# Three of every eight weighted one-hot rows on GpSimd instead of VectorE

## The reference, cut to what matters

```python
def one_block(args):
    x_blk, i_blk, g_blk = args
    u = jnp.take(peer_u, i_blk, axis=0)
    a = jax.nn.gelu(jnp.einsum("td,thkd->thk", x_blk, u)) * g_blk
    v = jnp.take(peer_v, i_blk, axis=0)
    return jnp.einsum("thk,thkd->td", a, v)
```

## Time and profile before

| | us |
|---|---|
| median of the runs | 3234.27 |
| lowest, highest run | 3233.52, 3235.56 |
| span of the profiled execution, first to last instruction | 3233.2 |
| VectorE busy in the span | 2188.2 (68%) |
| TensorE busy | 2442.6 (76%) |
| GpSimd busy | 823.7 (25%) |
| ScalarE busy | 1107.1 (34%) |

### The profile page before, as it was taken

The page is one execution under the profiler, slowest core; times in us unless marked ns, Lnnn a source line. Parts: engine busy times, 40 slices in busy tenths (PEclk is TensorE's granted clock), DMA queues, the critical chain, the costliest instruction groups (busy, mean ns, idle before and its releaser), DMA issues. The chain is left out here.

```text
span 3233.2 us, 30451 instructions
## 1 busy us (share of the span) xinstructions
PE 2442.6 (76%) x10473; PEld 1867.0 (58%) x10473; DVE 2188.2 (68%) x3036; ACT 1107.1 (34%) x1880; POOL 823.7 (25%) x571
## 2 busy tenths in 40 slices
PE   6896999999999999999999996000034005999994
PEld 5765787888888887888778796000023004444441
DVE  3698546545454555564545558999999999565668
ACT  4434235344343445454555442000089105000000
POOL 0200000000010100000000002777766773644444
PEclk9998599999999999999999998555555558999997
DMA  8452065565656555655435564999999996999998
GB/s 241 156 169 91 7 203 176 189 195 183 193 184 194 181 195 173 201 172 176 153 122 183 175 213 185 420 397 386 393 394 394 389 404 217 376 409 410 409 409 344
DMA packets 277587, 813.19 MB, mean 252 GB/s; under 512 B 32601, under 2 KB 40001, under 8 KB 243424
## 3 DMA queue, kind: packets, MB, share of 16 engines
q1 hardware_dynamic: 203504, 408.87, 37.9%
q0 software_dynamic: 73728, 402.69, 31.4%
q10 hardware_dynamic: 240, 0.18, 0.0%
HBM read 807.48 MB, written 4.19 MB: 251 GB/s over the span
## 5 line engine op out<-in xcount | busy, mean ns | idle before, releaser
L194 DVE TENSOR_TENSOR wl<-ring,wh 128x1024 fp32r<-128x1024 f32 (+2 forms) x616 | 738.9, 1241 | 647.1 <-ACT wh L189 644.5
L189 ACT CAST wh<-ring 128x1024 fp32r<-128x1024 f32 (+2 forms) x616 | 609.7, 1040 | 702.7 <-PE ps L210 649.1
L208 PE MATMUL ps<-wh,th 128*128 128x512 f32 (+1 forms) x1632 | 641.5, 393 | 28.8 <-DVE wl L194 21.6
L1805 POOL DMA_INDIRECT expert_rows<-in_peer_u,index x256 | 481.7, 1882 | 626.7 <-PE ps L1891 437.8
L210 PE MATMUL ps<-wh,tl 128*128 128x512 f32 (+1 forms) x1632 | 634.4, 389 | 0.0
L209 PE MATMUL ps<-wl,th 128*128 128x512 f32 (+1 forms) x1632 | 634.3, 389 | 0.0
L2195 DVE CUSTOM_DVE_ANT_0 junk<-expert_rows,h 128x2048 f32<-128x2048 f32 x256 | 570.1, 2287 | 6.0 <-DMA expert_rows<-in_peer_u,index 5.1
L2218 DVE SCALAR_TENSOR_TENSOR x_and_pieces<-expert_pieces,const,x_and_pieces 128x1024 f32<-128x1024 f32 x256 | 327.8, 1283 | 170.1 <-DMA expert_pieces<-in_peer_v,piece_index 87.2
L2278 PE MATMUL ps<-expert_slabs,by_expert 128*128 128x512 f32 x1024 | 439.7, 592 | 0.7 <-ACT by_expert L2319 0.7
L208 PEld LDWEIGHTS ps<-wh,th 128*128 128x128 f32 x1632 | 308.0, 189 | 101.8 <-DVE wl L194 31.8
L210 PEld LDWEIGHTS ps<-wh,tl 128*128 128x128 f32 x1632 | 307.7, 189 | 63.6
(11 more groups left out here) (332 smaller groups left out, 2748.5 us busy)
## 6 DMA issues: line engine op xcount, KB each, us to landing
ring<-in_w_in SPq DMA_DIRECT2D x112, 1024.0 KB, 5.1
ring<-in_w_up SPq DMA_DIRECT2D x64, 1024.0 KB, 5.3
ring<-in_w_down SPq DMA_DIRECT2D x64, 1024.0 KB, 5.0
expert_slabs<-in_peer_v SPq DMA_DIRECT2D x128, 512.0 KB, 6.8
ring<-in_w_out SPq DMA_DIRECT2D x32, 1024.0 KB, 5.0
ring<-in_w_peer_q SPq DMA_DIRECT2D x16, 1024.0 KB, 5.2
ring<-in_w_ukv SPq DMA_DIRECT2D x8, 1024.0 KB, 5.3
ring<-in_w_uq SPq DMA_DIRECT2D x8, 768.0 KB, 4.6
```

The costliest lines, as they stand in the source:

```text
L189: self.nc.scalar.copy(self.wh[:, i % 2, two, 0:w], self.ring[:, i, two, 0:w]).then_inc(self.high_ready, 1)
L194: self.nc.vector.tensor_tensor(self.wl[:, i % 2, two, 0:w], self.ring[:, i, two, 0:w], self.wh[:, i % 2, two, 0:w].bitcast(F32), ALU.subtr ...
L208: mm(o, hi, wh, start=start and k == 0, stop=False)
L1805: nc.gpsimd.indirect_dma_start(p.rows[:, n % GR, :], None, peer_u, bass.IndirectOffsetOnAxis(ap=p.index[:, n:n + 1], axis=0)).then_inc(p.l ...
```

## The change

Slots 2, 3 and 7 of each round of the second half are made by GpSimd, with the same instruction and operands as on VectorE. VectorE makes the other five. GpSimd makes its three rows of round r ahead of gather r, in the same queue, for r = 0 to 15; each row waits on `hot_used` for its four slots, and round 0 also for the turned weights (`columns`) and the index row (`iota_in`). TensorE waits for these slots on a semaphore of their own. The adds, the gathers' order and the first half are as they were.

```diff
+    POOL_ROWS = (2, 3, 7)
@@ gpsimd
+            def rows_by_pool(r):
+                if r == 0:
+                    pool.wait_ge(columns, 4)
+                    pool.wait_ge(iota_in, 16)
+                for i in POOL_ROWS:
+                    n = 8 * r + i
+                    pool.wait_ge(hot_used, P + n // 4 * 4 + 4)
+                    nc.gpsimd.tensor_scalar(row_hot[:, i, :], iota, turned_keys[:, 0, n:n + 1], turned_w[:, n:n + 1],
+                                            ALU.is_equal, ALU.mult).then_inc(rows_pooled, 1)
+
             for n in range(UNITS * TOPK):
+                if n < P // 8:
+                    rows_by_pool(n)
                 if n >= GR:
                     pool.wait_ge(piece_used, n - GR + 1)
                 nc.gpsimd.indirect_dma_start(
@@ vector, rows_by_vector
                 for n in range(at, at + 4):
-                    nc.vector.tensor_scalar(row_hot[:, n % 8, :], iota, turned_keys[:, 0, n:n + 1],
-                                            turned_w[:, n:n + 1], ALU.is_equal, ALU.mult).then_inc(rows_hot, 1)
+                    if n % 8 not in POOL_ROWS:
+                        nc.vector.tensor_scalar(row_hot[:, n % 8, :], iota, turned_keys[:, 0, n:n + 1],
+                                                turned_w[:, n:n + 1], ALU.is_equal, ALU.mult).then_inc(rows_hot, 1)
@@ tensor, spread
-                pe.wait_ge(rows_hot, g * 8 + (n + 1))
+                if half and i in POOL_ROWS:
+                    pe.wait_ge(rows_pooled, g * len(POOL_ROWS) + POOL_ROWS.index(i) + 1)
+                elif half:
+                    pe.wait_ge(rows_hot, P + g * (8 - len(POOL_ROWS)) + len([j for j in range(i + 1) if j not in POOL_ROWS]))
+                else:
+                    pe.wait_ge(rows_hot, g * 8 + (n + 1))
```

More of the change, by code:

```diff
@@ L2068, in peer_stage @@
          iota_in, sums_in, x_back, gain_in, added, sums, mean_ready, rooted, normed, stored, final, piece_used,
-         pieces_indexed, slab_used) = core.new(
+         pieces_indexed, slab_used, rows_pooled) = core.new(
             "dve_done", "rows_used", "shifted", "exponentiated", "gelued", "weighted", "picks_turned",
@@ L2072, in peer_stage @@
             "sums_in", "x_back", "gain_in", "x_added", "x_sums", "mean_ready", "rooted", "normed",
-            "stored", "final_steps", "pieces_used", "pieces_indexed", "expert_slabs_used")
+            "stored", "final_steps", "pieces_used", "pieces_indexed", "expert_slabs_used",
+            "rows_pooled")
         cols_hot = core.new("cols_hot_low", "cols_hot_high")
```

## The result

The changed kernel takes 3264.94 us (median of four runs, 3263.30 to 3268.07) against 3233.89 (3233.25 to 3235.56): 31.1 us slower, ratio 1.0095 with a 95% interval of 1.0081 to 1.0110. The way was forecast and the time lies within the stated range by 1 us, but the shift is 31.1 us where 13.6 were forecast.

The account below looks back on a forecast made before the run. The tail was taken as bound by bytes, its start set by the spread. Two rounds, 8.83 + 0.64 + 0.2 = 9.67 us, or 4.84 a round, end the spread 13.6 us later: 3234.3 + 13.6 = 3247.9, 3248 us; range 3240 to 3266.

Parts of the forecast that it names:

- The mechanism: In the spread, gathers queue behind GpSimd's rows and lose their lead, making a two-round loop of 4.84 us a round.
- The loop: From TensorE's last slot through row, gather, landing, add and VectorE's rows back to TensorE: 9.67 us for two rounds.
- The failed step: In the spread's loop: slot 7's GpSimd row costs 0.5 us, and slots 2 and 3 end about 0.2 us late.
- blocking of the gather: In the spread, a gather meeting a running VectorE add waits 0 to 1.28 us, mean 0.64.
- the gather's issue and landing: In the spread's loop: issue gap 0.30 us, then landing 4.2 us counted from the gather's start.
- VectorE and TensorE with the wake-ups: In the spread's loop: wake-up 0.1 us, VectorE's add, five rows and column compare 3.08, TensorE's last two slots 0.65.
- The price of a row: One 128x128 compare on GpSimd in the spread: taken as 0.5 us, between 0.32 and 0.75.
- The third rival: In the spread, serialised ports or rows of 1.3 us give 6.35 us a round, +34.8 us, 3269; chance 0.11.
- the landing loop: Spread rounds wait for each piece's DMA landing: 4.3 to 5.5 us a round, chance 0.76.
- The tail: Pieces and slabs after the spread: ends as far behind the spread as now, so everything moves by 13.6 us.
- The faster rival: Spread rounds take 3.79 us and the 9 us blocked gather at 2745.7 goes, gaining 8 us: 3225; chance 0.04.
- The Trainium skill's port rule: GpSimd operations reading SBUF and two-input VectorE ones block each other for a whole instruction; full exclusion over 6 us a round.

Follow-up runs that it names:

- e3: Against the kernel before: VectorE makes all eight rows, GpSimd none, but gather r still waits for TensorE's use of round r - 1's slots; 3252.62 us, +18.0.
- e1: Against the changed kernel: GpSimd's three rows of round r stand ahead of gather r + 7 instead of gather r; 3254.69 us, +20.1 over the kernel before.
- e2: Against the changed kernel: GpSimd's three rows of round r stand ahead of gather r + 1 instead of gather r; 3246.9 us, +12.3 over the kernel before.
- e6: Against the changed kernel: only slots 2 and 7 on GpSimd, rows of round r ahead of gather r + 1; 3237.9 us, +3.1 over the kernel before.
- e7: Against the kernel before: two tiny VectorE writes with waits ahead of each of the eight adds behind the spread; 3230.74 us, -4.1.

## Why the prediction was right in kind and wrong in size

**The mechanism held.** VectorE waits for each second piece (5.2 to 5.5 us), the loop spans two rounds, and e3 shows the order alone at +18.0 us. That the lead is lost was named as what decides.

**The loop was 12.3 us, not 9.67.** The failed step is the one that put only slot 7's row into it, at 0.5 us, with slots 2 and 3 "about 0.2 us late". It assumed evenly spaced rounds. They run in pairs: two adds close together, then a long wait. GpSimd is released by TensorE's slot 3 of the round behind a pair's first add, and all three rows stand in series ahead of the gather. By terms of the chain: rows 3.94 against 0.7, of which 2.36 is three rows of 0.79 and 1.6 their waits; blocking of the gather 0 against 0.64, as the add meets the row and not the gather; the gather's issue and landing 4.6 against 4.5; VectorE and TensorE with the wake-ups 3.8 against 3.83. That last agreement is chance: the path leaves VectorE after the add and one row, 1.5 us instead of 3.08, and TensorE's four slots take 2.06 us, in a stretch with a granted clock of 0.64 to 0.70, instead of the last two at 0.65. Sum 12.3 against 9.67.

**The price of a row** was 0.8 us, above the 0.75 that I took for the dear end. The 128x128 copy of 0.73 was probably near its own length; I had discounted a part as waiting.

**The third rival was nearer than the forecast, in part by chance.** "Much slower" priced dear rows and shared ports at 6.35 us a round; the measured round is 6.15. It kept the landing loop and put all three rows into it, at 3.1 us where 3.94 were measured. Its row of 1.3 us was too dear against 0.8, and its gather blocked for 1.28 us was not blocked; these errors cancel. Beside the loop there is the rows' own limit, GpSimd's round of 4.8 to 5.2 us, and it lies hidden: e1 and e2 uncover it, e6, with one row less, brings it down to 3.94. Since the limits hide each other, the +18 of the order and the +20 or +12 of the rows do not add up to 31.

**The tail held.** Spread's end to last add is 474.8 us against 474.1, as forecast, and the hole in the DMA is filled (304 GB/s for 121). The steps to it were not exact. Gather 15 is issued 6.1 us ahead of the spread's end instead of 3.6, and the next ones up to 22 follow at 1.6 us instead of 1.24, some of them held up beside adds (0.93 to 1.83 us each). That the pieces missing ahead and the earlier start of the DMA still cancel to 0.7 us is partly chance. The 32.3 us by which the spread ends later and this 0.7 are the 33.0 between the two spans; the profiled run of the changed kernel is the slowest of its four, hence 33.0 and not 31.1.

**The faster rival** was right that the hole at 2745 costs time: e7 gets 4.1 us back for it, half of the 8 that it put there. The change fills it as well, but pays for it with the longer spread.

**The Trainium skill's port rule** (SBUF — State Buffer, Two separate sides) agrees with rows of 0.8 us that take up to 2 where an add runs. It speaks of GpSimd operations that read SBUF; that a gather's issue is held up in the same way is read from e7 (8.91 to 0.94 us once the adds left gaps), not from the page. The rule of the Trainium skill's GPSIMD Engine Reference (Engine selection), near line rate for one-input work, doesn't describe a small one: 0.8 us, against the 0.1 estimated from it.

## What to carry to other kernels

Work given to an engine that looks idle is put in front of what its queue already issues; if that is a transfer that ran ahead, the lead is lost, and a hidden landing enters the loop. Keep the lead (issue ahead of the new work), then check that the engine's round, priced with its waits for the shared port, is below the bound that is to be relieved. And ask what the relieved engine's next limit is: here 0.06 us a round was all there was to win.

## What was not expected

- An indirect DMA's issue on GpSimd is stopped by VectorE adds that follow without a gap, and two tiny writes with waits, which leave 0.19 us between the adds, free it: 8.91 to 0.94 us.
- TensorE stood idle for 4 to 6 us once in two rounds of the changed kernel, and its granted clock from 2700 to 2760 was 0.64 to 0.70; with ten products put behind every second round it was 0.81 to 0.85. With one GpSimd row and no such products it was 0.84 from 2700 to 2740, with idle times of about 4 us.
- A gather's own duration is 1.03 us behind a row on GpSimd and 0.94 behind another gather, and the issue gap ahead of it 0.17 instead of 0.30 us.
